# Queries and keys of two self-attentions kept as high and low parts, and their logits made in three passes

## The chip, the core and the metric

The kernel runs on one core of a Trainium2 chip. The time is the device time of one launch in microseconds (us); lower is better. The profile comes from one further execution under the hardware profiler. The core's engines run side by side and meet at semaphores: PE (TensorE, matrix products; its weight loads are shown apart as PEld), DVE (VectorE), ACT (ScalarE), POOL (GpSimd) and SP (SyncE, which here issues the loads of weights).

## What is computed

Two transformer blocks in a row on one sequence of 256 tokens of 1024 features, all in float32. The change touches the logits of the self-attention of each block. In both there are 8 heads of 64 features. The first block:

```python
logits = jnp.einsum('bhqd,bhkd->bhqk', qb, kb).astype(jnp.float32) * scale
logits = logits + cum_f[:, :, qs:qe, None] - cum_f[:, :, None, :qe]
...
p = jax.nn.softmax(logits, axis=-1).astype(v.dtype)
outs.append(jnp.einsum('bhqk,bhkd->bhqd', p, vb))
```

The second block, with 256 tokens in one block of 256 keys, is plain causal attention with a linear bias:

```python
s_own = jnp.einsum('bhqd,bhld->bhql', qi, k_own).astype(jnp.float32) * scale
s_own = jnp.where((dist_own >= 0)[None, None],
                  s_own - slopes[None, :, None, None, None] * dist_own[None, None], -jnp.inf)
```

Around them stand projections, gates, a pooled and two convolved branches, a cross attention to 256 memory tokens, and two feed-forward layers.

## The kernel before

**Weights in units.** The weights are read from device memory in 248 units of 2 x 128 rows by 512 columns. SP loads a unit to `raw_ring` (four slots), ACT rounds it to the short float type into `hi_ring` (`hi`, L504), DVE subtracts to get the remainder into `lo_ring` (`lo`, L956), and PE multiplies. A product of two split operands is `three_passes` (L1791 to L1794): high times high, high times low, low times high, each a matmul with a weight load of its own, all added up in one bank of the accumulator. The activations (`h_hi_lo`, `memT_hi`, `branch_hi` and so on) are split too. Most matmuls of the kernel are such passes.

**Queries and keys.** They come out of PE transposed (features on partitions, tokens along the row): four groups of 128 features by 256 tokens, so that a group `g` holds two heads, `e` = 0 on partitions 0 to 63 and `e` = 1 on partitions 64 to 127. `take_half` (L541 on ACT, L1035 on DVE) copies two groups, 128 x 512, from a bank to `q_T` or `k_T` in plain float32. In the first block ACT and DVE copy one half each, in the second ACT copies both.

**Logits.** `score` (L2008) makes the logits of one head for one half of the tokens, with one plain float32 matmul (L2013) over 64 partitions: tokens 0 to 127 against keys 0 to 127 (128 columns), tokens 128 to 255 against all keys (256 columns). So a group is four calls (`parts`, L437): head 0 with 128 and 256 columns into one bank, then head 1 with 128 and 256 into the next. PE runs a plain float32 matmul as two instructions, each with a weight load. In the first block a one-pass matmul over 16 partitions (L2017) adds the forget term to each call.

**Where they stand.** The programs of all engines are written out by hand in a fixed order. In the first block the four calls of a group are spread inside one weight unit (`beside1`, L2050), after every second group of three passes, at the steps `ATT1_AT` (L55). In the second block the four calls of a group stand together between two weight units: `scores2` (L2245), called by `follow(0)`, `follow(1)`, `follow(6)` and `follow(7)`, behind the units `MEM_K1` + 0, + 1 and `GELU2` + 2, + 3. The first of them waits for the queries and the keys (`q2_out`, `k2_out`). The softmax behind a group runs on DVE (`take_scores`, L1079), ACT (`exponentials`, `normalize`) and PE again (`turn_prob`, L2027, six 128 x 128 transposes; `attend`, L2036, six matmul instructions for each head, the two heads on different columns of the array).

**What else DVE does there.** `conv_taps(n)` (L1398) does n of 62 multiply-adds of a convolution on 128 x 256 between the weight units, n from a table written in the code. `m.junk` (L377), where ACT throws away squares, is `gates[20:24]`.

## Time and profile before

| | |
|---|---|
| time, median of 3 runs (lowest, highest) | 810.21 us (810.2, 810.51) |
| the profiled execution's own time | 810.24 us |
| its span, from the first to the last instruction | 808.8 us |
| granted TensorE clock, mean | 0.999 of full speed |
| PE busy | 793.3 us, 98% |
| PE weight loads busy | 698.9 us, 86% |
| DVE busy | 570.8 us, 71% |
| ACT busy | 430.5 us, 53% |
| POOL busy | 90.3 us, 11% |
| read from device memory | 161.81 MB, 201 GB/s over the span |

The time of a launch is the span and some 1.4 us around it. Times in the trace are counted from the first instruction. A matmul's recorded duration holds the depth of the pipeline: matmuls follow each other faster than their durations, so what a matmul costs is read from the distance of starts, or from the chain, in which each piece reaches to the next.

### The profile page before, as it was taken

How to read it: one execution, taken by the hardware profiler on the slowest of the kernel's cores; microseconds unless marked ns; L12 is line 12 of the kernel's file. 1: busy time of each engine (PE TensorE's matmuls, PEld its weight loads, DVE VectorE, ACT ScalarE, POOL GpSimd, SP SyncE). 2: the span in 40 equal slices, each digit the busy share in tenths (PEclk: the TensorE clock that was granted, in tenths of full speed). 3: DMA queues.
4: the chain of work that ended last, by engine and by line, in shares of the span. 5: the costliest groups of instructions: out<-in, count | busy, mean ns of one | idle time of the engine just before them, and what ended most of it. 6: DMA issues, size and time to landing. Idle time of an engine off the chain costs nothing.

```text
span 808.8 us, 12246 instructions
## 1 busy us (share of the span) xinstructions
PE 793.3 (98%) x4868; PEld 698.9 (86%) x4868; DVE 570.8 (71%) x776; ACT 430.5 (53%) x642; POOL 90.3 (11%) x143
## 2 busy tenths in 40 slices
PE   6999999999989999999999999999999999999997
PEld 5999988899779888888889998788987988888885
DVE  5986987879977575656666989848556765656564
ACT  5554465564355655544556477547545644444452
POOL 4033960001210000000011000011001100000001
PEclk9999999999999999999999999999999999999999
DMA  9999876965637475566466554445433665666651
GB/s 320 367 281 324 334 247 227 360 247 190 231 95 241 146 234 185 181 191 194 162 208 205 166 155 154 156 160 201 162 103 105 187 203 183 189 196 185 186 180 53
DMA packets 83608, 163.65 MB, mean 202 GB/s; under 512 B 5456, under 2 KB 13840, under 8 KB 83552
## 3 DMA queue, kind: packets, MB, share of 16 engines
q1 hardware_dynamic: 81632, 157.31, 59.5%
q10 hardware_dynamic: 1424, 4.81, 1.8%
q0 software_dynamic: 496, 0.76, 0.5%
q8 instruction: 39, 0.64, 0.3%
q14 instruction: 17, 0.14, 0.0%
HBM read 161.81 MB, written 1.05 MB: 201 GB/s over the span
## 4 chain that ended last, share of the span: by engine, by line
PE 91%; DVE 2%; ACT 2%; issue 1%; DMA 1%; SPq 1%; POOL 1%; DVEq 0%; POOLq 0%; ACTq 0%
PE bank L1792 22%; PE bank L1794 21%; PE bank L1793 21%; PE bank L1823 13%; PE bank L1825 7%; PE bank L2013 1%; DMA raw_ring<-in_w_in 1%; PE bank L2366 1%; PE bank L2387 1%; PE bank L1863 1%; SPq L458 1%; ACT hi_ring L504 1%; DVE x_residual L1076 1%; PE bank L2017 1%; PE bank L2032 0%
## 5 line engine op out<-in xcount | busy, mean ns | idle before, releaser
L956 DVE TENSOR_TENSOR lo_ring<-raw_ring,hi_ring 128x1024 fp32r<-128x1024 f32 x248 | 306.3, 1240 | 159.4 <-ACT hi_ring L504 159.0
L504 ACT CAST hi_ring<-raw_ring 128x1024 fp32r<-128x1024 f32 x248 | 258.9, 1050 | 263.9 <-PE bank L1794 168.7
L1792 PE MATMUL bank<-h_hi_lo,hi_ring 128*128 128x256 f32 x560 | 163.7, 292 | 1.3 <-DVE h_hi_lo L1027 1.0
L1823 PE MATMUL bank<-h_hi_lo,hi_ring 128*128 128x512 f32 x448 | 158.7, 398 | 0.0
L1793 PE MATMUL bank<-h_hi_lo,hi_ring 128*128 128x256 f32 x560 | 158.3, 283 | 0.0
L1794 PE MATMUL bank<-h_hi_lo,lo_ring 128*128 128x256 f32 x560 | 158.3, 283 | 0.0
L1792 PE MATMUL bank<-hi_ring,branch_hi 128*128 128x512 f32 x320 | 126.5, 395 | 0.0
L1825 PE MATMUL bank<-h_hi_lo,lo_ring 128*128 128x256 f32 x448 | 125.8, 281 | 0.0
L1794 PE MATMUL bank<-hi_ring,branch_lo 128*128 128x512 f32 x320 | 124.8, 390 | 0.0
L1793 PE MATMUL bank<-lo_ring,branch_hi 128*128 128x512 f32 x320 | 124.6, 389 | 0.0
L1792 PEld LDWEIGHTS bank<-h_hi_lo,hi_ring 128*128 128x128 f32 x560 | 107.1, 191 | 5.0 <-issue 3.1
L1793 PEld LDWEIGHTS bank<-h_hi_lo,hi_ring 128*128 128x128 f32 x560 | 107.2, 192 | 0.5 <-issue 0.2
L1794 PEld LDWEIGHTS bank<-h_hi_lo,lo_ring 128*128 128x128 f32 x560 | 107.1, 191 | 0.0
L1823 PEld LDWEIGHTS bank<-h_hi_lo,hi_ring 128*128 128x128 f32 x448 | 84.2, 188 | 20.7
L1825 PEld LDWEIGHTS bank<-h_hi_lo,lo_ring 128*128 128x128 f32 x448 | 84.6, 189 | 0.5
L1794 PEld LDWEIGHTS bank<-hi_ring,branch_lo 128*128 128x128 f32 x320 | 60.1, 188 | 13.0
L1792 PEld LDWEIGHTS bank<-hi_ring,branch_hi 128*128 128x128 f32 x320 | 60.1, 188 | 12.9 <-issue 0.4
L1793 PEld LDWEIGHTS bank<-lo_ring,branch_hi 128*128 128x128 f32 x320 | 60.1, 188 | 12.1 <-issue 0.2
L1625 POOL TENSOR_SCALAR stat<-stat 128x1 f32<-128x1 f32 x10 | 3.3, 335 | 379.3 <-ACT gates L563 379.2
L1792 PE MATMUL bank<-hi_ring,h_hi_lo 128*128 128x512 f32 (+1 forms) x80 | 30.8, 385 | 0.3 <-ACT h_hi_lo L539 0.3
L1794 PE MATMUL bank<-hi_ring,h_hi_lo 128*128 128x512 f32 (+1 forms) x80 | 29.5, 369 | 0.0
L1793 PE MATMUL bank<-lo_ring,h_hi_lo 128*128 128x512 f32 (+1 forms) x80 | 29.5, 369 | 0.0
(273 smaller groups left out, 1041.7 us busy)
## 6 DMA issues: line engine op xcount, KB each, us to landing
raw_ring<-in_w_ff SPq DMA_DIRECT2D x128, 512.0 KB, 3.9
raw_ring<-in_w_in SPq DMA_DIRECT2D x64, 512.0 KB, 5.3
raw_ring<-in_w_out SPq DMA_DIRECT2D x16, 512.0 KB, 3.5
raw_ring<-in_w_xkv SPq DMA_DIRECT2D x16, 512.0 KB, 3.6
mem_v<-in_w_ada SPq DMA_DIRECT2D x12, 512.0 KB, 6.8
ada_ring<-in_w_ada SPq DMA_DIRECT2D x10, 512.0 KB, 5.3
mem_k<-in_w_ada SPq DMA_DIRECT2D x10, 512.0 KB, 6.7
raw_ring<-in_w_branch SPq DMA_DIRECT2D x8, 512.0 KB, 4.6
```

What stands on the lines that cost most here:

```text
L458: sp.dma_start(dst[:, :, i * S:i * S + S] if a < ADA_FIRST else dst.rearrange("p k n -> p (k n)"), src).then_inc(s.ada_in[slot], DMA)
L504: act.copy(m.hi[:, m.slot(u)], m.raw[:, m.slot(u)]).then_inc(s.hi_done, 1)
L956: dve.tensor_tensor(m.lo[:, m.slot(u)], m.raw[:, m.slot(u)], as_f32(m.hi[:, m.slot(u)]), ALU.subtract).then_inc(s.lo_done, 1)
L1076: dve.scalar_tensor_tensor(out=m.x[:, tt, cs], in0=m.norm[:, tt, cs], scalar=stat[:, 28 + tt:29 + tt], in1=m.x[:, tt, cs], op0=ALU.mult, o ...
L1792: pe.matmul(out, a_hi, b_hi, start=start, stop=False, skip_group_check=True)
L1793: pe.matmul(out, a_hi, b_lo, start=False, stop=False, skip_group_check=True)
L1794: return pe.matmul(out, a_lo, b_hi, start=False, stop=stop, skip_group_check=True)
L1823: pe.matmul(b, m.hi[:, slot, k, fc], x_both[:, k0 + k].rearrange("p a s -> p (a s)"), start=first and k == 0, stop=False, skip_group_check ...
L1825: mm = pe.matmul(b[:, 0:S], m.lo[:, slot, k, fc], x_both[:, k0 + k, 0, :], start=False, stop=last and k == UK - 1, skip_group_check=True)
L1863: ins = pe.transpose(ps(k)[:, tt * P:tt * P + P], src[:, tt, k * P:k * P + P], m.ident[:, :])
L2013: mm = pe.matmul(b[:, c0:c1], m.qT[rows, g, tt * P:tt * P + P], m.kT[rows, g, 0:c1 - c0], start=True, stop=not forget, skip_group_check=True)
L2017: mm = pe.matmul(b[:, c0:c1], m.pick[0:2 * NH, head:head + 1].to_broadcast([2 * NH, P]), m.key_sums[0:2 * NH, 0:c1 - c0], start=False, sto ...
```

## The change

Queries and keys are kept as a high part (rounded to the short float type) and a low part (what is left). ACT's `take_hi` copies both halves with rounding, for queries and for keys, in both blocks; DVE's `take_lo` waits for each half and subtracts it from the bank. A call of `score` becomes `three_passes` over 64 partitions, in place of one plain float32 matmul. Banks are given back one by one. The space: `q_lo` lies on the last four of the `gates`, `k_lo` on the second of two rows `post_rows`; so two loads of rows by ACT's queue are issued later, `b_ada` and `g_ff_post` behind the gates' column block 4 and not 3, `post_x_g_2` behind the unit `V2` + 3 and not `MEM_K0` + 3. The table of convolution taps beside the second attention is changed.

```diff
@@ -323,14 +324,21 @@
         self.mem_v = sb("mem_v", [NT, D])
-        gates = self.gates = sb("gates", [3 * KD, S])
-        self.qT = sb("q_T", [4, S])
-        self.kT = sb("k_T", [4, S])
+        with nc.sbuf_tensor("gates", [P, 3 * KD, S], F32) as all_gates:
+            gates = self.gates = all_gates[:, :, :]
+        sb("most_gates", [3 * KD - 4, S])
+        self.q_lo = sb("q_lo_T", [4, S], F32R)
+        self.q_hi = sb("q_hi_T", [4, S], F32R)
+        self.k_hi = sb("k_hi_T", [4, S], F32R)
         self.v_tok = sb("v_tok", [NT, NH * DH])
...
         probT = self.probT = sb("prob_T", [2, 512])
-        self.rows = sb("post_rows", [2, D])
+        with nc.sbuf_tensor("post_rows", [P, 2, D], F32) as rows:
+            self.rows = rows[:, :, :]
+        sb("leading_row", [D])
+        self.k_lo = sb("k_lo_T", [4, S], F32R)
         self.rowtmp = sb("row_tmp", [D])
@@ -543,6 +551,12 @@
+    def take_hi(u_end, b0, dst, sem):
+        act.wait_ge(s.used, u_end)
+        for i in range(2):
+            act.copy(pair(dst, 2 * i), bank[b0 + i][:, :]).then_inc(sem, 1)
     def take_mem(u_end, b0, dst):
@@ -630,9 +644,9 @@
         after(u)
-    take_half(14, 0, pair(m.qT, 0), s.q_out)
+    take_hi(14, 0, m.q_hi, s.q_hi)
     after(13)
-    take_half(15, 2, pair(m.kT, 0), s.k_out)
+    take_hi(15, 2, m.k_hi, s.k_hi)
     after(14)
@@ -677,7 +691,8 @@
                 act.copy(m.br_hi[:, 6:8, :], m.conv_y1).then_inc(s.mixers_hi, 1)
-        if c == 3:
+        if c == 4:
             act.wait_ge(s.gate_row, 4)
@@ -788,18 +803,16 @@
     take_mem(MEM_K0 + RING, 2, mem_keys(0))
-    load_row(m.rows[:, 1, :], "post_x_g_2", s.post_x_row_in)
     for j in range(RING):
...
         after(GLU2 + j)
-    for u0, dst, sem, b0 in ((Q2, m.qT, s.q2_out, 2), (K2, m.kT, s.k2_out, 0)):
+    for u0, dst, sem, b0 in ((Q2, m.q_hi, s.q2_hi, 2), (K2, m.k_hi, s.k2_hi, 0)):
         for j in range(RING):
             if j == RING - 1:
-                take_half(u0 + RING, b0, pair(dst, 0), sem)
-                take_half(u0 + RING, b0 + 1, pair(dst, 2), sem)
+                take_hi(u0 + RING, b0, dst, sem)
             after(u0 + j)
@@ -854,6 +867,7 @@
         follow(2 * RING + j)
+    load_row(m.rows[:, 1, :], "post_x_g_2", s.post_x_row_in)
     for j in range(RING):
@@ -1036,6 +1050,12 @@
+    def take_lo(hi_done, b0, hi, dst, sem):
+        for i in range(2):
+            dve.wait_ge(hi_done, i + 1)
+            dve.tensor_tensor(pair(dst, 2 * i), bank[b0 + i][:, :], as_f32(pair(hi, 2 * i)), ALU.subtract).then_inc(sem, 1)
     def ada_columns(ps_ok, done, b, n, at, b_at, gain=None):
@@ -1178,9 +1198,9 @@
     after(12)
-    take_half(14, 1, pair(m.qT, 2), s.q_out)
+    take_lo(s.q_hi, 0, m.q_hi, m.q_lo, s.q_out)
     after(13)
-    take_half(15, 3, pair(m.kT, 2), s.k_out)
+    take_lo(s.k_hi, 2, m.k_hi, m.k_lo, s.k_out)
@@ -1413,8 +1433,12 @@
     for j in range(2 * RING):
+        if j == RING - 1:
+            take_lo(s.q2_hi, 2, m.q_hi, m.q_lo, s.q2_out)
+        if j == 2 * RING - 1:
+            take_lo(s.k2_hi, 0, m.k_hi, m.k_lo, s.k2_out)
         after(Q2 + j)
-        conv_taps(5 - j % 2)
+        conv_taps((5, 4, 5, 3, 4, 3, 2, 3)[j])
     dve.wait_ge(s.dist_ok, 1)
@@ -1492,17 +1516,17 @@
         after(MEM_K1 + j)
-        conv_taps((0, 0, 4, 4)[j])
+        conv_taps((0, 2, 6, 5)[j])
     for j in range(RING):
...
         after(GELU2 + j)
-        conv_taps((3, 3, 0, 0)[j])
+        conv_taps((4, 3, 0, 0)[j])
     for j in range(RING):
...
         after(V2 + j)
-        conv_taps((1, 0, 1, 2)[j])
+        conv_taps((1, 0, 2, 2)[j])
     for j in range(RING):
@@ -2000,9 +2024,9 @@
             if u == 13:
-                free[0] = free[1] = s.q_out, 2
+                free[0], free[1] = (s.q_out, 1), (s.q_out, 2)
     free[5] = s.v_sum, 4
-    free[2] = free[3] = s.k_out, 2
+    free[2], free[3] = (s.k_out, 1), (s.k_out, 2)
     free[6] = free[7] = s.mixA_out, 2
@@ -2010,8 +2034,9 @@
         b = bank[banks[e]]
-        mm = pe.matmul(b[:, c0:c1], m.qT[rows, g, tt * P:tt * P + P], m.kT[rows, g, 0:c1 - c0], start=True,
-                       stop=not forget, skip_group_check=True)
+        tok, keys = slice(tt * P, tt * P + P), slice(0, c1 - c0)
+        mm = three_passes(b[:, c0:c1], m.q_hi[rows, g, tok], m.q_lo[rows, g, tok], m.k_hi[rows, g, keys],
+                          m.k_lo[rows, g, keys], True, not forget)
         if forget:
@@ -2233,11 +2258,11 @@
         features(Q2 + j, j, m.h_hi, m.h_lo, 2)
-    free[2] = free[3] = s.q2_out, 2
+    free[2], free[3] = (s.q2_out, 1), (s.q2_out, 2)
     claim(0, 1)
...
         features(K2 + j, j, m.h_hi, m.h_lo, 0)
-    free[0] = free[1] = s.k2_out, 2
+    free[0], free[1] = (s.k2_out, 1), (s.k2_out, 2)
```

**PE, the first logits of the second block.** The rows are PE's matmuls in program order between the last pass of unit `MEM_K1` + 0 (`memT_hi`, `lo_ring`) and the next unit; the sizes are weights' by moving columns. Before:

```order
L1794 MATMUL bank<-memT_hi,lo_ring 128x256
L2013 MATMUL bank<-k_T,q_T 128x128
L2013 MATMUL bank<-k_T,q_T 128x256
L2013 MATMUL bank<-k_T,q_T 128x128
L2013 MATMUL bank<-k_T,q_T 128x256
L1792 MATMUL bank<-memT_hi,hi_ring 128x256
```

and now, up to the first call of the second head:

```order
L1818 MATMUL bank<-memT_hi,lo_ring 128x256
L1816 MATMUL bank<-k_hi_T,q_hi_T 128x128
L1817 MATMUL bank<-k_lo_T,q_hi_T 128x128
L1818 MATMUL bank<-k_hi_T,q_lo_T 128x128
L1816 MATMUL bank<-k_hi_T,q_hi_T 128x256
L1817 MATMUL bank<-k_lo_T,q_hi_T 128x256
L1818 MATMUL bank<-k_hi_T,q_lo_T 128x256
L1816 MATMUL bank<-k_hi_T,q_hi_T 128x128
```

One row of `k_T,q_T` (two instructions in the trace) has become three rows, each one instruction: 12 where 8 ran. The second head's second and third pass, and its three passes of 256 columns, follow. The other three groups of the second block read the same.

**DVE, from the middle of the queries' units `Q2` to those first logits.** `L956` (now `L970`) makes the low part of a weight unit, `L1411` (now `L1431`) is a run of taps. Before:

```order
L1411 SCALAR_TENSOR_TENSOR mix<-pad_u,vector_columns,mix 128x256 x5
L956 TENSOR_TENSOR lo_ring<-raw_ring,hi_ring 128x1024
L1411 SCALAR_TENSOR_TENSOR mix<-pad_u,vector_columns,mix 128x256 x4
L956 TENSOR_TENSOR lo_ring<-raw_ring,hi_ring 128x1024
L1411 SCALAR_TENSOR_TENSOR mix<-pad_u,vector_columns,mix 128x256 x5
L956 TENSOR_TENSOR lo_ring<-raw_ring,hi_ring 128x1024
L1411 SCALAR_TENSOR_TENSOR mix<-pad_u,vector_columns,mix 128x256 x4
L956 TENSOR_TENSOR lo_ring<-raw_ring,hi_ring 128x1024
L1411 SCALAR_TENSOR_TENSOR mix<-pad_u,vector_columns,mix 128x256 x5
L956 TENSOR_TENSOR lo_ring<-raw_ring,hi_ring 128x1024
L1411 SCALAR_TENSOR_TENSOR mix<-pad_u,vector_columns,mix 128x256 x4
L1092 SCALAR_TENSOR_TENSOR gates<-neg_dist,bank 128x128
```

and now:

```order
L1057 TENSOR_TENSOR q_lo_T<-bank,q_hi_T 128x512 x2
L970 TENSOR_TENSOR lo_ring<-raw_ring,hi_ring 128x1024
L1431 SCALAR_TENSOR_TENSOR mix<-pad_u,vector_columns,mix 128x256 x3
L970 TENSOR_TENSOR lo_ring<-raw_ring,hi_ring 128x1024
L1431 SCALAR_TENSOR_TENSOR mix<-pad_u,vector_columns,mix 128x256 x4
L970 TENSOR_TENSOR lo_ring<-raw_ring,hi_ring 128x1024
L1431 SCALAR_TENSOR_TENSOR mix<-pad_u,vector_columns,mix 128x256 x3
L970 TENSOR_TENSOR lo_ring<-raw_ring,hi_ring 128x1024
L1431 SCALAR_TENSOR_TENSOR mix<-pad_u,vector_columns,mix 128x256 x2
L1057 TENSOR_TENSOR k_lo_T<-bank,k_hi_T 128x512 x2
L970 TENSOR_TENSOR lo_ring<-raw_ring,hi_ring 128x1024
L1431 SCALAR_TENSOR_TENSOR mix<-pad_u,vector_columns,mix 128x256 x3
```

Two subtractions for the queries and two for the keys have come in, and 7 of 36 taps have left this stretch (with the `Q2` units ahead of it); they stand further back, 5 in the next four units, and one more in each of `GELU2` and `V2`. In the first block `take_lo` stands where `take_half` stood, two rows for one, for queries and for keys.

## Rows read from the trace of the kernel before

**Rows 1.** The page: span, PE's busy time, and the chain's shares by engine.

```profile
span 808.8 us, 12246 instructions
...
PE 793.3 (98%) x4868; PEld 698.9 (86%) x4868; DVE 570.8 (71%) x776; ACT 430.5 (53%) x642; POOL 90.3 (11%) x143
...
PE 91%; DVE 2%; ACT 2%; issue 1%; DMA 1%; SPq 1%; POOL 1%; DVEq 0%; POOLq 0%; ACTq 0%
```

**Rows 2.** Waits of PE: waited for, us in total, times, longest.

```profile
PE bank L1928 <- DMA x_residual<-in_x: 5.2, 1, 5.2
...
PE bank L2044 <- ACT prob_T L591: 0.2, 1, 0.2
```

**Rows 3.** PE's groups by form: the logits' matmuls of 256 columns.

```profile
L2013 PE MATMUL bank<-k_T,q_T 64*128 64x256 f32 x32 | 8.0, 402 | 0.0
```

**Rows 4.** The chain at the first block's first logits: start, length (us), what.

```profile
86.51 0.12 PE bank L1794
86.63 0.42 PE bank L2013 x2
87.04 0.25 PE bank L2017
...
88.19 0.63 PE bank L2013 x2
88.82 0.31 PE bank L2017
```

**Rows 5.** The chain at the second block's first logits.

```profile
468.33 0.86 PE bank L2013 x8
```

**Rows 6.** Weight loads in order of time at a group of six transposes: start, length.

```profile
481.69 0.68 PEld L2032 LDWEIGHTS bank<-ident,gates 128*128 128x128 f32 x6
482.33 0.19 PEld L1792 LDWEIGHTS bank<-h_hi_lo,hi_ring 128*128 128x128 f32 x1
```

**Rows 7.** Weight loads in the first 0.1 us of the third logits (488.9:489.0).

```profile
488.93 0.20 PEld L2013 LDWEIGHTS bank<-k_T,q_T 64*128 64x128 f32 x2
```

**Rows 8.** Weight loads of the first `attend` of the second block.

```profile
508.25 0.19 PEld L2044 LDWEIGHTS bank<-gates,v_tok 128*64 128x64 f32 x2 [0.35 <-issue]
508.41 0.25 PEld L2045 LDWEIGHTS bank<-gates,v_tok 128*64 128x64 f32 x2
508.52 0.19 PEld L2044 LDWEIGHTS bank<-gates,v_tok 128*64 128x64 f32 x2
```

**Rows 9.** DVE's groups by form, 440 to 520 us.

```profile
L956 DVE TENSOR_TENSOR lo_ring<-raw_ring,hi_ring 128x1024 fp32r<-128x1024 f32 x24 | 29.3, 1221 | 7.0 <-ACT hi_ring L504 6.9
L1411 DVE SCALAR_TENSOR_TENSOR mix<-pad_u,vector_columns,mix 128x256 f32<-128x256 f32 x58 | 24.4, 481 | 0.0
...
L1120 DVE TENSOR_TENSOR branch_lo<-gates,branch_hi 128x512 fp32r<-128x512 f32 x1 | 0.7, 692 | 0.0
```

**Rows 10.** ACT, PE and DVE in order of time around the keys of the second block.

```profile
465.50 1.08 ACT L544 COPY k_T<-bank 128x512 f32<-128x512 f32 x2 [1.78 <-PE bank L1794]
...
465.30 0.28 PE L1792 MATMUL bank<-memT_hi,hi_ring 128*128 128x256 f32 x1
...
464.59 1.22 DVE L956 TENSOR_TENSOR lo_ring<-raw_ring,hi_ring 128x1024 fp32r<-128x1024 f32 x1
...
468.84 1.67 DVE L1411 SCALAR_TENSOR_TENSOR mix<-pad_u,vector_columns,mix 128x256 f32<-128x256 f32 x4
```

**Rows 11.** DVE in order of time: its idle stretches, in brackets.

```profile
70.33 0.24 DVE L1189 TENSOR_TENSOR forget_logits<-bank,b_f_row 128x8 f32<-128x8 f32 x2 [5.47 <-PE bank L1961]
...
482.61 1.23 DVE L956 TENSOR_TENSOR lo_ring<-raw_ring,hi_ring 128x1024 fp32r<-128x1024 f32 x1 [2.12 <-ACT hi_ring L504]
...
509.33 1.23 DVE L956 TENSOR_TENSOR lo_ring<-raw_ring,hi_ring 128x1024 fp32r<-128x1024 f32 x1 [1.10 <-ACT hi_ring L504]
```

**Rows 12.** ACT normalizes group 0; PE turns it.

```profile
479.19 1.48 ACT L586 ACTIVATE gates<-gates,softmax_stats 128x128 f32<-128x128 f32 x4
...
481.79 0.82 PE L2032 MATMUL bank<-ident,gates 128*128 128x128 f32 x6
```

More of the change, by code:

```diff
@@ L270, in __init__ @@
         self.mix_cols_ps, self.mix_cols = new("mix_cols_ps"), new("mix_cols")
-        self.q_out, self.k_out = new("q_out"), new("k_out")
+        self.q_hi, self.q_out, self.k_hi, self.k_out = new("q_hi"), new("q_out"), new("k_hi"), new("k_out")
         self.fl_ps, self.fl_out, self.fl_neg, self.fl_ln, self.nlogf = (
@@ L287, in __init__ @@
         self.glu, self.glu_sig = new("glu"), new("glu_sig")
-        self.q2_out, self.k2_out, self.v2_out = new("q2_out"), new("k2_out"), new("v2_out")
+        self.q2_hi, self.q2_out, self.k2_hi, self.k2_out = new("q2_hi"), new("q2_out"), new("k2_hi"), new("k2_out")
+        self.v2_out = new("v2_out")
         self.gelu_u, self.gelu_v, self.u_ok = new("gelu_u_in"), new("gelu_v"), new("gelu_u")
```

## The prediction

> **What bounds the kernel now.** I read the page first: PE is busy 793.3 of 808.8 us and holds 91% of the chain [rows 1]. Then PE's waits: the longest is 5.2 us for the input at the very start, and the shortest in the list 0.2 us [rows 2]. From the first block's logits on, PE runs nearly without a gap, so what the change adds to or takes from PE's own time counts in full, and work of ACT and DVE counts only where it makes PE wait. The chain gives the price of each call of the logits, since its pieces reach from one to the next [rows 4, 5]. The trace shows 32 instructions of 256 columns [rows 3]: 16 calls of two instructions; another 16 calls have 128 columns.
>
> **The prices on PE.** First what one pass of the split kind costs when it stands alone in a narrow part of the array. The forget term is such a pass, over 16 partitions: 0.25 us with 128 columns, 0.31 us with 256 [rows 4]. The difference, 0.06, is near the 0.053 us of 128 columns at 2.4 GHz, so 128 columns are not dearer per column than 256. The rest, 0.25 - 0.05 = 0.20 us, is the same for both: a weight load in the open and the emptying of the array. A weight load of 128 columns takes (482.33 - 481.69) / 6 = 0.107 us from start to start [rows 6], which leaves 0.09 for the emptying. Each further pass then adds the longer of its weight load and its columns: 0.108 us at 128 columns, where the columns alone would be 0.053, and 0.12 at 256, which is the distance of the weight units' passes [rows 4].
>
> First block, one call at a time:
> - 128 columns: 0.25 + 2 x 0.108 = 0.47 us, against 0.42 us now [rows 4]: +0.05.
> - 256 columns: 0.31 + 2 x 0.12 = 0.55 us, against 0.63 us [rows 4]: -0.08.
> - 8 calls of each: 8 x (0.05 - 0.08) = -0.24 us.
>
> Second block: four calls in a row. All 8 instructions take 0.86 us [rows 5], less than the 2 x (0.42 + 0.63) = 2.10 us of single calls, because the two heads lie on different halves of the rows and run side by side: two weight loads, each some 0.19 us long (as the last of [rows 6]), stand in 0.20 us, so they start within 0.02 us of each other [rows 7]. One head alone now costs 0.25 + 2 x 0.108 for its first three passes; the next three add 3 x 0.12, and the last has 128 columns more to stream, 0.05: 0.88 us. How far the two heads still overlap is the unknown, and the largest term:
> - Full overlap: 0.88 + 0.01 = 0.89 us for 0.86, +0.03, four times +0.12 us.
> - No overlap: the second head adds 3 x 0.108 + 3 x 0.12 = 0.68 us: 1.56, +0.70, four times +2.8 us.
> - Between them: the second head starts late because PE reaches ahead only so far in its program. `attend` has two heads of six weight loads and six matmuls on different columns, all waited for beforehand. The second head's first load (the second row of L2044) comes only at 508.52, 0.27 us after the first head's at 508.25, when that one has issued four loads [rows 8]. Now a head of logits has four loads and four matmuls, and its partner starts at once [rows 7]; after the change it has six and six, as `attend` has. If so, the second head's load goes out with the first head's fourth: 0.107 + 2 x 0.108 = 0.32 us. Then a group takes 0.88 + 0.32 = 1.20 us, +0.34, four times +1.36 us.
>
> I take the last, since `attend` is the nearest row in number of instructions, though it splits columns and not rows. PE in sum: -0.24 + 1.36 = +1.12 us.
>
> **ACT and DVE: hidden.** First block: DVE gets one subtraction more for queries and one for keys, 0.69 us each (the nearest form, 128 x 512, is the last of [rows 9]), ACT one copy of about 0.5 more for each, half of the 1.08 of two [rows 10]. They stand just ahead of a stretch in which DVE is idle for 5.47 us up to 70.33 [rows 11], and PE asks for these banks later still. Cost nothing; without that cover it would be 2 x 0.69 us, in the low parts of later units.
>
> Second block: ACT's two copies stay (465.50 to 466.58 for the keys [rows 10]). DVE's first subtraction can start at 466.1, and two of 0.69 end at 467.5, when `k2_out` is whole. PE wants it behind unit `MEM_K1` + 0, which starts at 465.30 [rows 10] and runs for 24 passes of 0.12, to 468.2. That is 0.7 us to spare. DVE has to be free at 466.1: it would not be in the old order, for it starts five taps at 465.7, behind `lo` at 464.59 [rows 10]. In the new order a unit has 3, 4, 3 and 2 taps at 0.40 from start to start, (1.67 - 0.48) / 3 of [rows 9, 10], and one low part of 1.22, 2.8 us at most for a unit of 2.88, so DVE keeps up with ACT, and its last two taps end at about 465.9. The queries have a whole slab of four units more.
>
> The taps moved back: the four more in `MEM_K1` + 1 and + 2 need 1.6 us, and DVE is idle 2.12 us there before 482.61 [rows 11]. The first group's probabilities are there at 479.19 + 1.48 = 480.67 and PE turns them at 481.79 [rows 12]; what DVE does for them is a reciprocal, and two taps stand ahead of it that did not, 0.8 us, less than the 1.1 between. Then DVE has two taps more without idle time, so it is 0.8 us late until its idle 1.10 us before 509.33 [rows 11] takes that up. What is late by 0.8 us there is low parts of weight units, and they have room: the one at 464.59 to 465.81 [rows 10] is for `MEM_K1` + 2, which PE starts two units, 5.8 us, after 465.30. The later loads of rows cost nothing either, their rows are used tens of us later. I put all this at 0; the bound upward is a wait at the keys, below.
>
> **Sum.** 810.24 + 1.12 = 811.36 us for the profiled execution; the median of the runs, 810.21, is 0.03 below it, so 811.3 us. That is +0.14%, within the 0.2% (1.62 us) that a measurement of this kernel can tell from no change.
>
> **The rivals.**
> - Full overlap (chance 0.16): -0.24 + 0.12 = -0.12, 810.1 us. For it: [rows 7] and the small lag of 0.02. Against it: `attend` [rows 8].
> - One head after the other (0.12): -0.24 + 2.8 = +2.56, 812.8 us, slower. In this kernel it would be the reach of PE's queue again, with a reach shorter than the passes of the first head. For it: 12 instructions instead of 8 stand before the second head's. Against it: `attend`'s heads overlap, only late. It decides from a lag of about 0.44 us for each group, where the sum passes 1.62. The Trainium skill, "TensorE: Matmul & The Clock Gate", part 3, "What overlaps and what doesn't", says that matmuls start and end strictly in program order and only weight loads are drawn ahead; by that the second head could not begin before the first has issued all its passes. The trace does not agree for the kernel before: the heads' loads alternate [rows 8], and 8 matmuls fit in 0.86 us [rows 5].
> - Columns alone count (0.05), if weights of the split kind hide behind each other in half the array: 128 columns 0.25 + 2 x 0.053 = 0.36, 256 columns 0.31 + 2 x 0.107 = 0.52; first block 8 x (-0.06 - 0.11) = -1.4, second, fully overlapped, 4 x (0.25 + 2 x 0.053 + 3 x 0.107 - 0.86) = -0.7: -2.1, 808.1 us, faster. Against it: the loads of 0.107 apart [rows 6]. The Trainium skill, "FP8 and Floating Point Precision", "TensorE Precision Notes", counts a true float32 product as four passes, and three stand against it here; that rule alone would give three quarters of the streaming time, this rival's direction.
> - The keys' low part late (0.10): at 468.2 PE waits for `k2_out`. The place is DVE: `take_lo` stands behind two taps and is waited for at once. It costs what exceeds 0.7 us; from 1.2 us late it turns my sum to slower. Price with DVE three taps and a low part behind, 2.4 us: 2.4 - 0.7 = 1.7, 813.0 us. Against it: the count above.
> - The forecast (0.51), and 0.06 for what I don't see, half to each side.
>
> **How the numbers follow.** Slower by over 0.2%: one head after the other 0.12, half of the late keys 0.05, 0.03 for a forecast whose lag is dearer than 0.44, 0.03 unseen: 0.23. Faster: columns alone 0.05, 0.03 unseen: 0.08. The rest, 0.69, within 0.2%. The range takes in full overlap below (810.1) and one head after the other above (812.8) with a little for a run's spread: 809.8 to 812.9.
>
> **What would show it.** In the first block a call of 128 columns with 0.47 and one of 256 with 0.55 in the chain before L2017 (now three lines); in the second four blocks of about 1.20 us, with the second head's first weight load 0.32 us behind the first's. Full overlap shows as a lag of 0.02 and 0.89 us, none as 1.56. No wait of PE for `k_lo_T`, and the unit after each group starting right behind it. It is wrong if PE waits for DVE at 468, if the three passes stand closer than 0.108 at 128 columns, or if time moves outside the two attentions.

## The result and the profile after

The changed kernel takes 811.91 us, the median of 17 runs, against 810.46 us for the kernel before, also of 17; the ratio is 1.0018, with a 95% interval of 1.0012 to 1.0025. One of the 17 runs fell in a slower state, with 868.89 us at a granted clock of 0.851, and is left out of the ratio. The change costs 1.45 us: a small loss, inside the 0.2% (1.62 us) that was forecast as "no change", though the interval reaches a little beyond it. The profiled execution took 811.61 us, with a span of 810.1 us. Its page, busy time and instructions of each engine:

```profile
span 810.1 us, 12318 instructions
...
PE 794.4 (98%) x4900; PEld 702.8 (87%) x4900; DVE 574.6 (71%) x782; ACT 431.3 (53%) x644; POOL 91.0 (11%) x143
```

PE has 32 matmuls more and 1.1 us more of busy time than in [rows 1], DVE six instructions more, ACT two. Most of the 1.3 us of span is PE's own. PE's list of waits has no new entry: the longest is again the input at the start, and neither `k_lo_T` nor `q_lo_T` is in it; the 0.2 us for `prob_T` in [rows 2] is gone.

```profile
PE bank L1952 <- DMA x_residual<-in_x: 5.5, 1, 5.5
```

The first block's logits, in the chain of the changed kernel (start, length, what), against [rows 4]. The three passes are L1816, L1817 and L1818; the forget term is L2042:

```profile
86.67 0.25 PE bank L1816
86.93 0.11 PE bank L1817
87.04 0.11 PE bank L1818
87.15 0.25 PE bank L2042
...
88.31 0.31 PE bank L1816
88.63 0.12 PE bank L1817
88.75 0.12 PE bank L1818
88.87 0.31 PE bank L2042
```

A call of 128 columns is 0.25 + 0.11 + 0.11 = 0.47 us, one of 256 is 0.31 + 0.12 + 0.12 = 0.55, both as forecast. The second block's first logits, the weight loads in order of time, against [rows 7]:

```profile
468.43 0.18 PEld L1816 LDWEIGHTS bank<-k_hi_T,q_hi_T 64*128 64x128 f32 x1
468.54 0.19 PEld L1817 LDWEIGHTS bank<-k_lo_T,q_hi_T 64*128 64x128 f32 x1
468.65 0.19 PEld L1818 LDWEIGHTS bank<-k_hi_T,q_lo_T 64*128 64x128 f32 x1
468.72 0.24 PEld L1816 LDWEIGHTS bank<-k_hi_T,q_hi_T 64*128 64x128 f32 x2
```

The first three loads stand alone. The fourth row is two loads within 0.05 us: the second head's first, 0.282 us behind the first head's, and the first head's fourth. From the first load to the next unit's first, a group takes 1.169, 1.164, 1.168 and 1.163 us, where the kernel before takes 0.862 or 0.863; forecast were 1.20 against 0.86.

To see where the time went I took PE's weight loads of both traces, left out those of queries and keys, and compared load number n with load number n. After minus before is +0.23 us at the first load behind the input (5.1 us; the input came later in that execution), +0.04 at 84 us, -0.08 at 165 us (the first block's logits), +0.18 at 283 us, +0.17 at 468 us, and +1.37 at 494 us, where it stays to the end. So there are three steps and not two: -0.13, **+0.29 between 232 and 283 us, where the change touches nothing**, and +1.20. ACT in order of time near 274 us, first in the kernel before, then in the changed one; the bracket is ACT's idle time ahead of the row:

```profile
273.55 0.18 ACT L511 ACTIVATION_READ_ACCUMULATOR gates<-gates 128x1 f32 x1
274.81 1.16 ACT L516 ACTIVATE gates<-gates,stat 128x1024 f32<-128x1024 f32 x1 [1.08 <-POOL stat L1605]
```

```profile
273.44 0.18 ACT L519 ACTIVATION_READ_ACCUMULATOR gates<-gates 128x1 f32 x1
274.99 1.15 ACT L524 ACTIVATE gates<-gates,stat 128x1024 f32<-128x1024 f32 x1 [1.37 <-POOL stat L1629]
```

POOL's step between the two rows has the same length in both. The 0.29 us lie between ACT's wait and its next instruction: 0.063 us from the wait's row to the scaling's before, 0.351 after. The scaling is that of the memory's rows; behind it in ACT's queue stand a second one, the copies of `branch_hi` and the high part of the next weight unit, then DVE's low part of it, which ends at 282.47 us before and at 282.65 after. PE's first weight load of that unit starts 0.12 us behind this end in both traces. The profile files the idle time of the changed kernel under "issue", but the equal distance says that PE waits for the low part. The load in the kernel before, then in the changed one:

```profile
282.58 0.19 PEld L1792 LDWEIGHTS bank<-hi_ring,branch_hi 128*128 128x128 f32 x1
```

```profile
282.76 0.19 PEld L1816 LDWEIGHTS bank<-hi_ring,branch_hi 128*128 128x128 f32 x1 [0.36 <-issue]
```

So at this place the chain by ACT ends last, by a hair in the kernel before and by 0.3 us in the changed one, and what ACT loses there counts in full: the loads step by 0.29 us at this unit.

### The profile page after: what moved, and what is told of

It reads as the page before. It is cut to its first block, busy times and chain, and to the rows that moved or that the text cites. A ratio compares the mean times of both kernels' runs of the same rounds, so it can differ in the third digit from the quotient of the medians.

```text
span 810.1 us, 12318 instructions
## 1 busy us (share of the span) xinstructions
PE 794.4 (98%) x4900; PEld 702.8 (87%) x4900; DVE 574.6 (71%) x782; ACT 431.3 (53%) x644; POOL 91.0 (11%) x143
## 4 chain that ended last, share of the span: by engine, by line
PE 91%; DVE 2%; ACT 2%; issue 1%; DMA 1%; SPq 1%; POOL 1%; ACTq 0%; DVEq 0%; POOLq 0%
PE bank L1816 23%; PE bank L1817 21%; PE bank L1818 21%; PE bank L1847 13%; PE bank L1849 7%; DMA raw_ring<-in_w_in 1%; PE bank L2391 1%; PE bank L2412 1%; PE bank L1887 1%; SPq L466 1%; ACT hi_ring L512 1%; DVE x_residual L1096 1%; PE bank L2042 1%; PE bank L2057 0%; DVE ada_acc L1002 0%
## 5 line engine op out<-in xcount | busy, mean ns | idle before, releaser
L970 DVE TENSOR_TENSOR lo_ring<-raw_ring,hi_ring 128x1024 fp32r<-128x1024 f32 x248 | 306.1, 1239 | 157.5 <-ACT hi_ring L512 156.7
L1816 PE MATMUL bank<-h_hi_lo,hi_ring 128*128 128x256 f32 x560 | 163.8, 292 | 1.3 <-DVE h_hi_lo L1041 1.0
L1817 PE MATMUL bank<-h_hi_lo,hi_ring 128*128 128x256 f32 x560 | 158.4, 283 | 0.0
L1818 PE MATMUL bank<-h_hi_lo,lo_ring 128*128 128x256 f32 x560 | 158.3, 283 | 0.0
L1816 PE MATMUL bank<-hi_ring,branch_hi 128*128 128x512 f32 x320 | 126.6, 396 | 0.1
L1818 PE MATMUL bank<-hi_ring,branch_lo 128*128 128x512 f32 x320 | 124.8, 390 | 0.0
L1817 PE MATMUL bank<-lo_ring,branch_hi 128*128 128x512 f32 x320 | 124.6, 389 | 0.0
L1816 PEld LDWEIGHTS bank<-h_hi_lo,hi_ring 128*128 128x128 f32 x560 | 107.1, 191 | 4.9 <-issue 2.7
L1817 PEld LDWEIGHTS bank<-h_hi_lo,hi_ring 128*128 128x128 f32 x560 | 107.3, 192 | 0.5 <-issue 0.2
L1818 PEld LDWEIGHTS bank<-h_hi_lo,lo_ring 128*128 128x128 f32 x560 | 107.2, 191 | 0.0
L1816 PEld LDWEIGHTS bank<-hi_ring,branch_hi 128*128 128x128 f32 x320 | 60.1, 188 | 13.2 <-issue 0.8
L1818 PEld LDWEIGHTS bank<-hi_ring,branch_lo 128*128 128x128 f32 x320 | 60.1, 188 | 13.0
L1817 PEld LDWEIGHTS bank<-lo_ring,branch_hi 128*128 128x128 f32 x320 | 60.1, 188 | 12.1 <-issue 0.2
L1816 PE MATMUL bank<-hi_ring,h_hi_lo 128*128 128x512 f32 (+1 forms) x80 | 30.7, 384 | 0.2 <-ACT h_hi_lo L547 0.2
L1817 PE MATMUL bank<-lo_ring,h_hi_lo 128*128 128x512 f32 (+1 forms) x80 | 29.5, 369 | 0.0
L1818 PE MATMUL bank<-hi_ring,h_hi_lo 128*128 128x512 f32 (+1 forms) x80 | 29.5, 369 | 0.0
```

The lines of the kernel that those rows point to most:

```text
L970: dve.tensor_tensor(m.lo[:, m.slot(u)], m.raw[:, m.slot(u)], as_f32(m.hi[:, m.slot(u)]), ALU.subtract).then_inc(s.lo_done, 1)
L1816: pe.matmul(out, a_hi, b_hi, start=start, stop=False, skip_group_check=True)
L1817: pe.matmul(out, a_hi, b_lo, start=False, stop=False, skip_group_check=True)
L1818: return pe.matmul(out, a_lo, b_hi, start=False, stop=stop, skip_group_check=True)
```

## The experiments

**1. The second block's heads, pass by pass by turns.**

```
-        for i in range(4):
-            score(a, g, banks, False, i)
+        for tt in range(2):
+            pairs = [args(tt), args(2 + tt)]
+            for p, (qi, ki) in enumerate(((1, 3), (1, 4), (2, 3))):
+                for x in pairs:
+                    mm = pe.matmul(x[0], x[qi], x[ki], start=(p == 0), stop=(p == 2), ...)
```

> The changed kernel, but in the second block the two heads of a group are written by turns, pass by pass (first head's first pass, second head's first pass, and so on); in the first block nothing differs. Theory (PE reaches ahead only over a few instructions, so a head that stands behind six of its partner's starts late): the second head's first weight load comes 0.01 to 0.02 us behind the first head's, where it came 0.28 us behind, and the distance from a group's first weight load to that of the unit behind it falls from 1.17 us to 0.89 us; four groups give back 1.1 us, so a median of 810.8 us where the changed kernel has 811.91. Rival (two heads of split passes hinder each other, whatever their order): the lag vanishes but the group keeps 1.1 us or more, and the median stays at 811.8. Rival (the cost is not in the groups): the same median.

Measured: 810.83 us (11 runs) beside 810.3 for the kernel before, ratio 1.0005 (0.9996 to 1.0014). Weight loads at the first group, then the chain there:

```profile
468.33 0.19 PEld L2059 LDWEIGHTS bank<-k_hi_T,q_hi_T 64*128 64x128 f32 x2
468.44 0.19 PEld L2059 LDWEIGHTS bank<-k_lo_T,q_hi_T 64*128 64x128 f32 x2
```

```profile
468.40 0.89 PE bank L2059 x12
```

Each row is now two loads in 0.19 us: the second head's comes 0.004 us behind. The group is 0.884 us in all four places, so the same twelve passes cost 0.02 us more than the eight instructions of before. Both rivals fall: the 1.2 us were the order in which the heads are written.

**2. Five passes a head, and eight.** The same loop as in the changed kernel, head after head, with the number of passes of a call as a parameter: two and three, or four and four.

```
+            n = (2, 3)[tt]      # the other kernel: (4, 4)[tt]
+            factors = ((m.q_hi, m.k_hi), (m.q_hi, m.k_lo), (m.q_lo, m.k_hi), (m.q_lo, m.k_lo))[0:n]
+            for p, (q, k) in enumerate(factors):
```

> The changed kernel with the third pass (queries' low part by keys' high part) left out of the 128-column call of each head in the second block, so that a head has five passes and not six; that part of the product is missing from the result. Theory (a count: the second head's first weight load can go out when no more than three matmuls of the first are still to be issued, as the changed kernel's 0.28 us with six and the 0.01 us of the kernel before with four both say): it goes out with the first head's second matmul, 0.16 us behind the first head's first load. Rival (a fixed lag of split passes, or one that belongs to a full queue and not to a count): it stays at 0.28 us, or falls to 0.01 us.

> The changed kernel with a fourth pass (low part by low part) in every call of the second block, eight passes a head; it adds work that the reference does not need. Theory (a count of three unissued matmuls): the second head's first load goes out when the first head has issued its fifth matmul, which alone is 0.16 + 3 x 0.115 = 0.50 us behind the first load; a group then takes 1.17 + 0.22 + 0.11 + 0.12 = about 1.6 us. Rival (fixed lag): 0.28 us, and 1.4 us for a group. Rival (columns alone matter): the group grows by 0.16 us only.

Measured: 810.74 and 813.81 us, one run each. Weight loads of the first group with five passes, then with eight; a row with x2 begins with the second head's first load or has it in it:

```profile
468.38 0.18 PEld L2057 LDWEIGHTS bank<-k_hi_T,q_hi_T 64*128 64x128 f32 x1
468.49 0.19 PEld L2057 LDWEIGHTS bank<-k_lo_T,q_hi_T 64*128 64x128 f32 x1
468.56 0.23 PEld L2057 LDWEIGHTS bank<-k_hi_T,q_hi_T 64*128 64x128 f32 x2
```

```profile
468.81 0.18 PEld L2057 LDWEIGHTS bank<-k_hi_T,q_hi_T 64*128 64x128 f32 x1
...
469.13 0.19 PEld L2057 LDWEIGHTS bank<-k_lo_T,q_lo_T 64*128 64x128 f32 x1
469.25 0.25 PEld L2057 LDWEIGHTS bank<-k_hi_T,q_hi_T 64*128 64x128 f32 x2
```

The lag is 0.171 us with five (expected 0.16) and 0.506 with eight (0.50), and the group of eight passes a head takes 1.619 us (about 1.6). A fixed lag is out. By the number of the first head's matmuls the lag is 0.013 us (four, the kernel before), 0.171 (five), 0.282 (six, the changed kernel) and 0.506 (eight): the second head starts when three matmuls of the first are still to be issued.

**3. Calls by turns.** Only the order of calls is changed, each with its three passes together.

```
-        for i in range(4):
+        for i in (0, 2, 1, 3):
             score(a, g, banks, False, i)
```

> The changed kernel, with only the order of the second block's calls changed: first head 128 columns, second head 128, first head 256, second head 256, three passes each. Theory (a count of three unissued matmuls): the second head's first load has only three before it and goes out 0.00 to 0.02 us behind the first; the first head's next call stands behind three of the other and goes on in time, so a group takes 0.88 to 0.95 us. Rival (it needs turns pass by pass): 1.0 us or more for a group.

Measured: 810.72 us, one run. The first loads, the same first row as by turns of passes:

```profile
468.59 0.19 PEld L1816 LDWEIGHTS bank<-k_hi_T,q_hi_T 64*128 64x128 f32 x2
```

The lag is 0.010 us and a group takes 0.891. A change of order in one line brings what turns pass by pass bring, within 0.007 us a group, as the count says.

**4. The taps as they were.**

```
-        conv_taps((5, 4, 5, 3, 4, 3, 2, 3)[j])
+        conv_taps(5 - j % 2)
```

(and the three tables behind it, back to those of the kernel before)

> The changed kernel with DVE's taps laid out as in the kernel before (5 and 4 by turns beside the units of queries and keys, 36 in all where the change has 29). Theory (the spare time of 0.86 us at the keys is bought by moving the taps): DVE is still at its taps when ACT has made the keys' high part, and its two subtractions end after PE wants them; PE waits for the keys' low part at the first logits of the second block, 0.7 us if only the keys' subtractions are late, 2.0 us if the queries' 1.3 us are still owed too, and the median is 812.6 to 814 us. Rival (there was spare time enough for both): no wait of PE there, and 811.9 us as the changed kernel.

Measured: 813.0 us (5 runs), ratio 1.0037 (1.0024 to 1.0051), 1.1 us above the changed kernel. DVE in order of time around the keys, then PE's list of waits:

```profile
466.55 2.08 DVE L1431 SCALAR_TENSOR_TENSOR mix<-pad_u,vector_columns,mix 128x256 f32<-128x256 f32 x5
468.52 1.29 DVE L1057 TENSOR_TENSOR k_lo_T<-bank,k_hi_T 128x512 fp32r<-128x512 f32 x2
```

```profile
PE bank L1816 <- DVE k_lo_T L1057: 1.3, 1, 1.3
```

Five taps stand ahead of the keys' subtractions, which end at 469.82; PE loads at 469.93. The wait of 1.3 us lies between the 0.7 and the 2.0 that were expected for the two cases. In the changed kernel the same two rows are:

```profile
465.22 0.87 DVE L1431 SCALAR_TENSOR_TENSOR mix<-pad_u,vector_columns,mix 128x256 f32<-128x256 f32 x2
466.29 1.29 DVE L1057 TENSOR_TENSOR k_lo_T<-bank,k_hi_T 128x512 fp32r<-128x512 f32 x2 [0.19 <-ACT k_hi_T L558]
```

There DVE waits 0.19 us for ACT, and is done at 467.57, 0.86 us before PE's 468.43. The moved taps are what makes the split form's extra work free here.

**5. ACT's place: one instruction more, and the kernel before with two more.** An ACT copy near 70 us is written in pieces, which moves all later ACT instructions back by one (on top of experiment 1) or by two (in the kernel before, which has two fewer than the changed one).

```
-    take_half(16, 6, pair(mix, 0), s.mixA_out)
+    act.wait_ge(s.used, 16)
+    act.copy(pair(mix, 0)[:, 0:256], bank[6][:, 0:256])
+    act.copy(pair(mix, 0)[:, 256:512], bank[6][:, 256:512]).then_inc(s.mixA_out, 1)
```

> The kernel with passes by turns, and one ACT copy of 512 columns near 70 us (mixA's first half) written as two of 256, so that every later ACT instruction stands one place further back; nothing else differs. Theory (ACT pays about 0.29 us at every 128th of its instructions when it comes right behind a wait; in the changed kernel two more ACT copies move the 320th onto the scaling of the normalized rows, which PE waits for): the gap from the end of the semaphore's wait to that scaling near 275 us falls from 0.35 us to 0.06 us, the jump of 0.29 to 0.30 us against the kernel before between 232 and 282 us is gone, and the median is 810.5 us against the 810.83 of passes by turns. Rival (the 0.29 us belong to something else in the change, such as a row load or the memory's layout): gap and time stay.

> The kernel before, with the same ACT copy written as three (256, 128 and 128 columns), so that every later ACT instruction stands two places further back, as in the changed kernel; nothing else of the change is in it. Theory (place in ACT's program): the gap ahead of the scaling near 275 us is 0.35 us where the kernel before has 0.06, and the median is 0.29 us above before, 810.6. Rival (it needs the rest of the change): the gap stays at 0.06 us and the median at 810.3.

Measured: 810.42 us (11 runs, ratio 1.0000, 0.9991 to 1.0009) and 810.76 (11 runs, ratio 1.0004, 0.9996 to 1.0013), beside 810.49 for the kernel before. The medians move the expected way, by 0.41 us down from experiment 1 (0.60, each taken against the kernel before beside it) and by 0.27 up from the kernel before, but the intervals are wider than that, so the traces decide. The scaling near 274 us, first with one more, then in the kernel before with two more:

```profile
274.56 1.15 ACT L524 ACTIVATE gates<-gates,stat 128x1024 f32<-128x1024 f32 x1 [1.08 <-POOL stat L1631]
```

```profile
275.20 1.15 ACT L516 ACTIVATE gates<-gates,stat 128x1024 f32<-128x1024 f32 x1 [1.37 <-POOL stat L1608]
```

The idle time is 1.08 us where it was 1.37, and 1.37 where it was 1.08. PE's loads tell the same: between 232 and 283 us the distance to the kernel before grows by 0.28 us in the kernel before with two more, by 0.30 in experiment 1, and by 0.03 with one more. The rest of the change isn't needed for it.

**6. Both heads at once in the first block too, at two places.** A call there stood alone among a unit's weight passes; now the two heads' calls go out together, then their forget terms.

```
-            if i % 2 == 0:
-                score(s.att1, here, (4, 5), True, i // 2)
+            if i % 4 == 0:
+                score_pass((4, 5), here, (i // 4,), True, s.att1)
```

`score_pass` runs over the three passes and, inside them, over the two heads; a loop over the heads' forget terms follows.

> Passes by turns in both blocks: in the first block the two heads' calls of 128 columns go out together at the unit's first place and the two of 256 together at its fifth, pass by pass by turns, and then the two forget terms. Theory (a call standing alone among weight passes pays for an empty array and an open weight load, and two heads on different halves of the rows pay it once): a pair of 128 columns takes 0.84 us from its first load to the unit's next, where two calls alone take 2 x 0.73, and a pair of 256 takes 0.98 for 2 x 0.85; 4 x 1.34 = 5.4 us less than passes by turns, 805.4 us. Rival (weights become the bound once PE is ahead; the margin was 0.06 to 0.15 us near 203 and 222 us): part of it is lost there, 807 to 808 us.

Measured: 803.81 us (4 runs), ratio 0.9918 (0.9905 to 0.9932). The chain at the first pair of 128 columns and the first of 256:

```profile
86.70 0.48 PE bank L2056 x6
87.18 0.36 PE bank L2063 x2
...
89.15 0.55 PE bank L2056 x6
89.70 0.42 PE bank L2063 x2
```

From its first load to the unit's next a pair takes 0.842 and 0.975 us, as expected, but the gain over experiment 1 is 7.0 us and not 5.4, in the medians and in the loads between 84 and 165 us alike. I had left out how a call begins: its first load comes 0.325 us behind the load before it, where a unit's own come 0.12 behind each other (the changed kernel's trace at 88 us), so each place that is given up saves 0.2 us more, 8 x 0.2 = 1.6 us. The rival, weights that come late, does not appear: between 165 and 232 us the distance of the loads stays within 0.03 us.

**7. All at one place.**

```
-            if i % 4 == 0:
-                score_pass((4, 5), here, (i // 4,), True, s.att1)
+            if i == 0:
+                score_pass((4, 5), here, (0, 1), True, s.att1)
```

> As passes by turns in both blocks, with all four calls of a group of the first block at one place, the unit's first, and the four forget terms behind them. Theory: 0.88 us to the first forget term's load, as in the second block, 0.33 for three more and 0.31 to the unit's next: 1.53 us for a group, where two places take 1.82; 4 x 0.29 = 1.2 us less, 804.2 us. Rival (weights or the softmax become the bound): as slow as two places, or slower.

Measured: 802.04 us (4 runs), ratio 0.9896 (0.9882 to 0.9909). This kernel computes wrong logits, for the start mark of the 256-column call falls while the sums of the 128-column call in the same bank are still open; it is of use for its time alone. The first group takes the expected 1.53 us. With the start of a place, 4 x 0.2 us, on top of the expected 1.2, the gain over two places would be 2.0 us; the medians differ by 1.77 and the loads between 84 and 165 us by 1.78. The missing 0.2 us is not traced here. The next two kernels leave out the second start mark and compute the right logits:

```
-                                   start=(p == 0), ...
+                                   start=(p == 0 and (tt == 0 or not forget)), ...
```

> All four calls of a group of the first block at one place, pass by pass by turns, as in the run before, but only the 128-column call starts its bank anew; the 256-column call's first pass into the same bank no longer carries the start mark. In the run before both carried it while the 128-column sums were still open for their forget term, and its result was not the reference's. Theory (the mark costs no time): the same 1.53 us for a group and the same median, 802.0 us. Rival (that run was fast because it did something else): slower, toward 804.

> The same with one ACT copy near 70 us written as two, as in the run that moved ACT's 320th instruction off the scaling of the normalized rows. Theory (ACT's place): 0.29 us less, 801.7 us. Rival (with PE 9 us ahead another work ends last there, so ACT's 0.29 us is hidden or comes back): 802.0 us.

Measured: 801.74 us (4 runs), ratio 0.9895 (0.9879 to 0.9912), and 801.61 us (4 runs), ratio 0.9893 (0.9878 to 0.9908). The mark costs nothing. The medians of the two differ by 0.13 us, which these runs can't tell from nothing, but the traces show ACT's shifted place. The scaling, in the first of the two and in the second:

```profile
266.25 1.15 ACT L524 ACTIVATE gates<-gates,stat 128x1024 f32<-128x1024 f32 x1 [1.37 <-POOL stat L1629]
```

```profile
265.88 1.15 ACT L524 ACTIVATE gates<-gates,stat 128x1024 f32<-128x1024 f32 x1 [1.08 <-POOL stat L1631]
```

PE's loads, compared one by one, step by the whole 0.29 us at the unit that waited at 282 us in the changed kernel, and the gain stays to the end. So the rival, that another work ends last there once PE is 9 us ahead, falls too. The chain of the first of the two at the first group:

```profile
86.63 0.89 PE bank L2056 x12
87.52 0.65 PE bank L2063 x4
```

**8. The kernel before with all four calls at one place.** Full float32, one start mark for a bank, then the four forget terms. The calls keep their old order, head after head (`parts`): with four matmuls a head, both heads start together without turns.

```
+    def scores_forget(a, g, banks):
+        for e, tt, c0, c1 in parts():
+            pe.matmul(..., m.qT[rows, g, ...], m.kT[rows, g, ...], start=(tt == 0), stop=False, ...)
```

> The kernel before (queries and keys in full float32, no low parts), with all four calls of a group of the first block at the unit's first place and the four forget terms behind them, one start mark for each bank; the second block as it was. Theory (the order is worth the time, not the split form): a group of eight takes 0.86 us to the first forget term's load and 1.51 us to the unit's next, for 2 x (0.67 + 0.93) us and three more entries of 0.2 us: 4 x 2.3 = 9.2 us less than before, 801.2 us, 0.5 us below the split form in the same order. Rival (the gain needs the split form): above 803 us.

Measured: 801.18 us (4 runs), ratio 0.9888 (0.9873 to 0.9903), the lowest median of all. Its chain at the first group:

```profile
86.59 0.86 PE bank L2026 x8
87.45 0.65 PE bank L2030 x4
```

Eight instructions of float32 in 0.86 us, twelve passes of the split form in 0.89: with both heads together the form of the product is worth nothing on PE, and the split form has DVE's and ACT's extra work besides. In the medians the split form at one place is 0.56 us slower, in the loads 0.43 from 84 us on: some 0.08 in each block, and 0.27 at the unit behind ACT's scaling.

## Why the prediction was right, and where it was not

The forecast was 811.3 us in a range of 809.8 to 812.9; the median is 811.91. Term by term, with the steps of the loads in the traces:

- **First block, -0.24 us: right in mechanism, too large in size; measured -0.13.** Both call times came out as forecast. The error is in the sum: 0.47 against 0.42 and 0.55 against 0.63 are differences of rounded rows, taken eight times, and the 0.05 of a call of 128 columns is 0.062. By the weight loads, from a call's first to the unit's next, they are 0.727 against 0.665 and 0.853 against 0.933, 8 x (0.062 - 0.080) = -0.14.
- **Second block, +1.36 us: right in mechanism, 0.16 too large; measured +1.20.** The second head starts late because PE reaches ahead over few instructions. The `attend` rows [rows 8] were the right neighbour, and experiments 1 to 3 show the count. The lag is 0.28 and not 0.32: the second head goes out when the first's third matmul is issued, at 0.277, and not with its fourth load, at 0.33. Full overlap and one head after the other are both out for this order; full overlap is what either order by turns gives.
- **The Trainium skill's rule on order** ("TensorE: Matmul & The Clock Gate", Part 3, "What overlaps and what doesn't") fails in this trace too: the second head's first matmul starts at 468.718, ahead of the first head's fourth at 468.824, which stands before it in the program. Such starts, and the 0.86 us for eight matmuls, contradict the rule; the alternating loads that I also named against it in the prediction do not, since it lets loads go ahead. The same part, "The mechanism", gives PE a reorder window of 64 entries, out of which a weight load for other rows is drawn ahead of running matmuls. By that the second head's first load would go out at once; with six passes ahead of it it waits 0.28 us, so the reach that counts here is far shorter.
- **Keys' low part late, 0.10: did not happen**, with 0.86 us to spare where I had 0.7. Experiment 4 shows that the place was rightly named: with the old taps PE waits 1.3 us there. That count of DVE's taps was the prediction's most useful zero.
- **"ACT ... Cost nothing": this step failed, by 0.29 us.** I priced ACT's two copies in the first block by their time, which is hidden. Their number is not: they move every later ACT instruction by two, and at 275 us that exposes 0.29 us on the path. Experiment 5 takes it away and puts it into the kernel before. The forecast's last sign of being wrong, "if time moves outside the two attentions", is what caught it: the total is inside the range, but by that sign this part of the forecast is wrong.

Sum: -0.13 + 1.20 + 0.29 = +1.36 us, and the spans differ by 1.3 us; the input also came 0.2 us earlier in the profiled execution of before, of which 0.04 is left at 84 us. The forecast was +1.12 us. The miss of 0.24 is ACT's 0.29 and the first block's 0.11, less the 0.16 by which the second block was overestimated: that the last stood against the others was luck. The medians differ by 1.45 us, the rest is within the spread. That 811.91 is 0.6 us above 811.3 has one more reason: the kernel before itself came out 0.25 us higher over 17 runs (810.46) than over the three that the forecast started from (810.21).

What stays open: why ACT pauses. The traces show where (below). The profile's page lists two DMA queues of the kind "instruction", and one of them, q14, moves a packet of 8,192 bytes within 2.1 us of each of ACT's instructions number 64, 192, 320 and so on to 832, in the kernel before and in the changed one. Half-way between (128, 256 and so on to 896) the nearest such packet is over 8 us away at six places of seven. So the pause most likely belongs to the fetching of ACT's instructions. It isn't a wait for that packet to land, for where the pause shows, the packet starts 0.65 to 2.1 us behind the paused instruction. No run here separates the fetching from another cause that counts instructions.

## What to carry to other kernels

Two chains of small matmuls on different halves of the rows start together only if the second is near enough in the program, here behind no more than four matmuls of the first: write them by turns, call by call at least. A place at which small matmuls stand among larger ones has a price of its own, here some 0.45 us (experiment 7 gives up four such places for 1.8 us), so gather such calls in one place before making each cheaper. And compare two traces by the same instruction's time all along the run: the steps show where time goes, also where the change has no line.

## What the runs showed of the hardware

- **PE's reach.** With four, five, six and eight matmuls of the first head ahead of it, the second head's first load comes 0.013, 0.171, 0.282 and 0.506 us behind the first head's, each time when three matmuls of the first are unissued, 0.005 to 0.012 us behind the start of the one before those three. With three ahead of it (calls by turns) it comes after 0.010 us. `attend` in the kernel before, with heads on different columns, shows the same count: of six matmuls the first head's third starts at 508.517 us, the second head's first at 508.523.
- **Every 128th of ACT's instructions, from number 64 on.** Counted with its waits, ACT's instructions number 192, 320, 576 and 832 start 0.34 to 0.35 us behind the wait ahead of them, where others start 0.06 behind it, if they come right behind a wait: numbers 192 and 576 in the kernel before, 192, 320 and 832 in the changed one. Numbers 448 and 704 are themselves a wait or stand behind a running instruction, and nothing shows. With one ACT copy more (experiment 5) number 448 comes right behind a wait, and pauses 0.34 us, while numbers 384, 512 and 640, which do so too, start 0.06 behind it. Of the 170 or so instructions that come behind a wait on an idle ACT, only two or three others in these two kernels start more than 0.08 us behind it, all of them roundings of weights near 250 and 287 us.
- **Price of a form.** Alone among others, a call in the split form costs 0.06 us more at 128 columns and 0.08 less at 256 than float32; eight of float32 or twelve of the split form, with two heads side by side, take 0.863 and 0.884 us.
